# Gates, MoBA's queries and keys and cross attention's queries and keys as one 512-column matmul per weight tile

## What is computed

```
h = rmsnorm(x)
q_a,k_a,v_a, q_b,k_b,v_b, z, xbc, dt = split(h @ w_in)
y_a = sliding window attention(q_a,k_a,v_a)      # RoPE, sinks
y_b = MoBA attention(q_b,k_b,v_b)                # one block of 256: causal
y_c = SSD mixer(z, xbc, dt)                      # conv, scan, gated norm
g_a,g_b,g_c = split(sigmoid(h @ w_gate + b_gate))
x += (g_a*(y_a@w_br_a) + g_b*(y_b@w_br_b) + g_c*(y_c@w_br_c)) @ w_mix_out
q = rmsnorm(x) @ w_cq;  k,v = split(rmsnorm(mem) @ w_ckv)
x += softmax(q k^T) v @ w_co                     # 4 heads, 256 memory tokens
x += relu(rmsnorm(x) @ w_up)^2 @ w_down
```

## Time and profile before

| | us |
|---|---|
| median of 3 runs | 1207.43 (1206.92 to 1207.82) |
| the profiled execution, its time | 1205.99 |
| the same, span of the profile | 1204.2 |
| PE busy | 1168.9 (97%) |
| PE weight loads busy | 1047.6 (87%) |
| DVE busy | 774.5 (64%) |
| ACT busy | 573.3 (48%) |
| POOL busy | 66.1 (5%) |

### The profile page before, as it was taken

One profiled execution on the slowest core, in us unless ns is written; L12 is line 12 of the kernel. 1 busy time (PEld: TensorE's weight loads), 2 busy tenths in 40 slices (PEclk: granted clock), 3 DMA queues, 4 the chain that ended last, 5 costly groups with the idle time before them and its releaser, 6 DMA issues. The chain is left out here.

```text
span 1204.2 us, 18337 instructions
## 1 busy us (share of the span) xinstructions
PE 1168.9 (97%) x7503; PEld 1047.6 (87%) x7503; DVE 774.5 (64%) x1172; ACT 573.3 (48%) x808; POOL 66.1 (5%) x93
## 2 busy tenths in 40 slices
PE   4999999999999999999999999999999999999997
PEld 3998899999998887888889888999989988888886
DVE  5877765886654456656568677568685445655655
ACT  5545454534554355344355545544455444534443
POOL 2000001410000000000000000043000000000000
PEclk9999999999999999999999999999999999999999
DMA  5743525746643445655636533366655443575560
GB/s 183 229 156 110 171 71 179 232 137 218 199 165 133 154 148 188 210 175 176 209 109 209 175 126 120 112 186 193 204 182 190 152 148 105 175 243 168 190 220 36
DMA packets 156412, 201.31 MB, mean 167 GB/s; under 512 B 7152, under 2 KB 111912, under 8 KB 156328
## 3 DMA queue, kind: packets, MB, share of 16 engines
q1 hardware_dynamic: 155296, 199.46, 51.0%
q10 hardware_dynamic: 1032, 0.67, 0.2%
HBM read 199.04 MB, written 1.08 MB: 166 GB/s over the span
## 5 line engine op out<-in xcount | busy, mean ns | idle before, releaser
L1401 DVE TENSOR_TENSOR w_lo<-raw,w_hi 128x2048 fp32r<-128x2048 f32 (+1 forms) x184 | 412.5, 2245 | 249.6 <-ACT w_hi L742 249.5
L742 ACT ACTIVATE w_hi<-raw 128x2048 fp32r<-128x2048 f32 (+1 forms) x184 | 343.2, 1875 | 108.4 <-PE psum L1114 78.5
L1097 PE MATMUL psum<-act_both,w_hi 128*128 128x256 f32 x832 | 240.9, 290 | 0.0
L1099 PE MATMUL psum<-act_both,w_lo 128*128 128x256 f32 x832 | 235.2, 283 | 0.0
L1098 PE MATMUL psum<-act_both,w_hi 128*128 128x256 f32 x832 | 235.2, 283 | 0.0
L1085 PE MATMUL psum<-act_both,w_hi 128*128 128x512 f32 x512 | 181.8, 399 | 2.3 <-DVE w_lo L1401 2.3
L1097 PEld LDWEIGHTS psum<-act_both,w_hi 128*128 128x128 f32 x832 | 159.3, 191 | 1.1 <-issue 0.5
L1098 PEld LDWEIGHTS psum<-act_both,w_hi 128*128 128x128 f32 x832 | 159.4, 192 | 0.6 <-issue 0.5
L1099 PEld LDWEIGHTS psum<-act_both,w_lo 128*128 128x128 f32 x832 | 159.2, 191 | 0.0
L1086 PE MATMUL psum<-act_both,w_lo 128*128 128x256 f32 x512 | 143.5, 280 | 0.0
L1085 PEld LDWEIGHTS psum<-act_both,w_hi 128*128 128x128 f32 x512 | 96.1, 188 | 27.2 <-DVE w_lo L1401 3.1
(11 more groups left out here) (252 smaller groups left out, 1923.9 us busy)
## 6 DMA issues: line engine op xcount, KB each, us to landing
raw<-in_w_in_dram SPq DMA_DIRECT2D x35, 1024.0 KB, 5.0
raw<-in_w_up_dram SPq DMA_DIRECT2D x32, 1024.0 KB, 5.4
raw<-in_w_down_dram SPq DMA_DIRECT2D x32, 1024.0 KB, 4.9
raw<-in_w_gate_dram SPq DMA_DIRECT2D x24, 1024.0 KB, 7.1
raw<-in_w_ckv_dram SPq DMA_DIRECT2D x16, 1024.0 KB, 5.2
raw<-in_w_br_ssd_dram SPq DMA_DIRECT2D x8, 1024.0 KB, 10.0
raw<-in_w_mix_out_dram SPq DMA_DIRECT2D x8, 1024.0 KB, 5.0
raw<-in_w_cq_dram SPq DMA_DIRECT2D x8, 1024.0 KB, 5.3
```

The costliest lines, as they stand in the source:

```text
L742: act.activation(w_hi[:, slot, 0:n], raw[:, slot, 0:n], ACT.Copy).then_inc(hi_ready.sem, 1)
L1097: pe.matmul(dst, m_hi[:, k, cs], a_hi[:, k, :], start=k == 0, stop=False)
L1099: ins = pe.matmul(dst, m_lo[:, k, cs], a_hi[:, k, :], start=False, stop=k == kt - 1)
L1401: dve.tensor_tensor(w_lo[:, slot, 0:n], raw[:, slot, 0:n], w_hi[:, slot, 0:n].bitcast(F32), ALU.subtract).then_inc(lo_ready.sem, 1)
```

## The change

Four kinds of unit, 24 of them per layer (`qkb` 4, `gate` 12, `kx` 4, `qx` 4), take the form of the up-projection: 16 pairs of matmuls (512 columns and 256) in place of 48 matmuls of 256 columns, and two banks per unit in place of one. After such a unit ACT copies the second halves of both banks into the destination (for a gate it adds half the bias and multiplies by 0.5 on the way), DVE adds the first halves (two instructions of 256 columns) and frees both banks. A gate's tanh is a third instruction on ACT, of 512 columns in SBUF, and comes after `hi` of the unit three further on and before the exponentials of the slot. `xbc` and `branch_c` keep the old form. The two halves of the memory's activations become one tile at the same place.

```diff
+MERGED = ('qkb', 'gate', 'kx', 'qx')
 def unit_banks(u, w):
...
-    if w["kind"] == "up":
+    if w["kind"] == "up" or w["kind"] in MERGED:
         return [(u, m) for m in range(2)]
...
+        hm_both = at("hm_both", [P, 2, KT, SEQ], F32R, r_c)
+        hm_hi, hm_lo = hm_both[:, 0], hm_both[:, 1]
...
                 act.wait_ge(*unit_done.at(l, u + 1))
-                if kind == "qkb":
+                if kind in MERGED:
+                    if kind == "gate":
+                        branch, tile = w["col"] // D, (w["col"] % D) // P
+                        if branch == 1:
+                            act.wait_ge(*is_read(l, (U_BRA + 1, 1)))
+                        if branch == 2:
+                            act.wait_ge(*is_read(l, (U_BRB + 1, 1)))
+                    for m in range(2):
+                        src = bank((u, m))[:, SEQ:2 * SEQ]
+                        if kind == "gate":
+                            b0 = PC_BGATE + branch * KT + tile + m
+                            ins = act.activation(g_sb[:, tile + m, :], src, ACT.Identity, bias=half[:, l, b0:b0 + 1],
+                                                 scale=0.5)
+                        else:
+                            dst = {"qkb": qkT_b, "kx": k_xT, "qx": q_xT}[kind]
+                            ins = act.activation(dst[:, 2 * j + m, :], src, ACT.Copy)
+                    ins.then_inc(half_out.sem, 1)
+                elif kind == "qkb":
...
                     if u + RING < NU and w["kind"] != "xbc":
                         hi(l, u + RING)
+                    if w["kind"] == "gate" and "gate" in MERGED:
+                        c = (w["col"] % D) // P
+                        for m in range(2):
+                            act.wait_ge(*is_read(l, (u, m)))
+                        act.activation(g_sb[:, c:c + 2, :], g_sb[:, c:c + 2, :], ACT.Tanh).then_inc(gate_out.sem, 1)
...
+                elif w["kind"] in MERGED:
+                    both = hm_both if w["act"] == "mem" else act_both
+                    for m in range(2):
...
+                            pe.matmul(dst, m_hi[:, k, cs], both[:, :, k, :], start=k == 0, stop=False)
                             ins = pe.matmul(dst[:, 0:SEQ], m_lo[:, k, cs], a_hi[:, k, :], start=False,
                                             stop=k == kt - 1)
...
+                if kind in MERGED:
+                    n = merged_until(u)
+                    dve.wait_ge(*half_out.at(l, n))
+                    for m in range(2):
+                        src = bank((u, m))[:, 0:SEQ]
+                        if kind == "gate":
+                            dst = g_sb[:, (w["col"] % D) // P + m, :]
+                            ins = dve.scalar_tensor_tensor(dst, src, 0.5, dst, ALU.mult, ALU.add)
+                        else:
+                            dst = {"qkb": qkT_b, "kx": k_xT, "qx": q_xT}[kind][:, 2 * j + m, :]
+                            ins = dve.tensor_tensor(dst, dst, src, ALU.add)
+                        ins.then_inc(free((u, m)), 1)
+                    return
```

More of the change, by code:

```diff
@@ L360, in trunk @@
         yc_lo = at("yc_lo", [P, KT, SEQ], F32R, r_c + 8192)
-        hm_hi = at("hm_hi", [P, KT, SEQ], F32R, r_c)
-        hm_lo = at("hm_lo", [P, KT, SEQ], F32R, r_c + 8192)
+        hm_both = at("hm_both", [P, 2, KT, SEQ], F32R, r_c)
+        hm_hi, hm_lo = hm_both[:, 0], hm_both[:, 1]
         r_d = region(8192)
@@ L478, in trunk @@
         close_hi = Signal(sem("close_hi"), 8)
+        n_merged = sum(w["kind"] in MERGED for w in UNITS)
+        gate_out = Signal(sem("gate_out"), 12)
+        half_out = Signal(sem("half_out"), n_merged)
         mg_ready = Signal(sem("mg_ready"), 4)
@@ L571, in prev_user, with merged_until @@
             return u - RING
+        def merged_until(u):
+            return sum(w["kind"] in MERGED for w in UNITS[:u + 1])
         def unit_bank(u, i):
@@ L1027, in _ @@
             operands = {"h": (act_hi, act_lo), "merged": (act_hi, act_lo), "hq": (act_hi, act_lo),
-                        "hf": (act_hi, act_lo), "mem": (hm_hi[:], hm_lo[:]), "o": (o_hi[:], o_lo[:]),
+                        "hf": (act_hi, act_lo), "mem": (hm_hi, hm_lo), "o": (o_hi[:], o_lo[:]),
                         "y_swa": (ya_hi[:], ya_lo[:]), "y_moba": (yb_hi[:], yb_lo[:]),
@@ L1085, in unit @@
                             pe.matmul(dst, m_hi[:, k, cs], act_both[:, :, k, :], start=k == 0, stop=False)
+                            ins = pe.matmul(dst[:, 0:SEQ], m_lo[:, k, cs], a_hi[:, k, :], start=False,
+                                            stop=k == kt - 1)
+                elif w["kind"] in MERGED:
+                    both = hm_both if w["act"] == "mem" else act_both
+                    for m in range(2):
+                        if m == 1:
+                            inner(l, u)
+                        dst, cs = bank(unit_bank(u, m)), slice(m * P, (m + 1) * P)
+                        for k in range(kt):
+                            if turned and m == 0 and k % 2 == 0:
+                                pe.wait_ge(*is_read(l, ("norm", turned, k // 2)))
+                            pe.matmul(dst, m_hi[:, k, cs], both[:, :, k, :], start=k == 0, stop=False)
                             ins = pe.matmul(dst[:, 0:SEQ], m_lo[:, k, cs], a_hi[:, k, :], start=False,
@@ L1213, in job_scores @@
                 if n == 8:
-                    wait_read(pe, l, [(first_of("qkb", i), 0) for i in range(4)] + [unit_bank(U_VB, t) for t in range(TT)])
+                    wait_read(pe, l, [key for i in range(4) for key in unit_banks(first_of("qkb", i), UNITS[first_of("qkb", i)])] + [unit_bank(U_VB, t) for t in range(TT)])
                 for i in range(2):
@@ L1278, in cross_scores @@
                 key = ("xscore", h)
-                wait_read(pe, l, ([(U_KX + i, 0) for i in range(4)] if h == 0 else []) + [(U_QX + h, 0)])
+                wait_read(pe, l, [key for v in ([U_KX + i for i in range(4)] if h == 0 else []) + [U_QX + h]
+                                   for key in unit_banks(v, UNITS[v])])
                 pe.wait_ge(*is_free(l, key))
@@ L1628, in evacuate @@
                         if i == 0:
-                            wait_read(dve, l, [(v, 0) for v in range(u - 8, u) if UNITS[v]["kind"] == "gate"])
+                            if "gate" in MERGED:
+                                dve.wait_ge(*gate_out.at(l, 4 * (1 + ("branch_a", "branch_b", "branch_c").index(kind))))
+                            else:
+                                wait_read(dve, l, [(v, 0) for v in range(u - 8, u) if UNITS[v]["kind"] == "gate"])
                         if kind == "branch_a":
```

## The result

The changed kernel takes 1212.05 us (median of 6 executions) against 1207.09 for the kernel before beside it; the ratio is 1.0040, 95% interval 1.0026 to 1.0054. It is 0.4% slower. One of the six executions took 1641.11 us at a granted clock of 0.657 and is not in the ratio; the other five have a median of 1211.30 and a mean of 1211.84. The profiled execution took 1211.1 us with a span of 1209.3, where the one of before took 1205.99 with a span of 1204.2.

A forecast was written before the change was run, and what follows sets the result against it. The prediction took PE to bound the kernel. Per layer, waits of 0.85 + 2.6 us less 2.6 saved gave +0.85, so +1.7 for two layers on the 1207.43 us median: 1209.1 us, range 1204.6 to 1214.0.

The forecast's parts named there:

- The likeliest case: Both bank waits come and outweigh the savings: 1209.1 us, own range 1205.2 to 1211.5, chance 0.56.
- wait at `kva`: After unit 2, `kva` needs both `qa` banks and waits for the second token tile's RoPE copy: 0.85 us per layer.
- later start of unit 34, from unit 29 on: Bank wait for `branch_b1`, DVE's additions and a share for POOL meetings: 2.6 us per layer, between 2.27 and 3.6.
- savings of the other units: Twenty units per layer, all but 2, 29, 30 and 33, each save 0.13 us: 2.6 us.
- two paces: Up-projection units take 5.55 or 5.65 us; the saving per changed unit was put between 0.07 and 0.21 us.
- Unit 34's bank wait: Unit 34 needs banks 2 and 3 and waits for DVE's last read of `branch_b1`: 2.27 us computed per layer.
- the bank alone: At unit 34, the wait for bank 3 even with nothing later on DVE: 1.46 us.
- the late exponentials: In slots 28 and 29 tanh waits for DVE's additions, shifting exponentials and POOL's multiplication; a meeting costs about 1.30 us.
- SSD's chain becomes the bound: Exponentials wait behind tanh and POOL's multiplications fall on DVE's masks: 4.9 us slower, 1212.3 us, chance 0.30.
- one meeting before, at the scaling: In the kernel before, POOL's slot 28 multiplication overlapped DVE's `y_tok` scaling: 1.30 us beside 1.51.
- two rivals: Slower ones: SSD's chain as bound, 1212.3 us, chance 0.30; PE's time by columns alone, 1214.3 us, chance 0.05.
- the gap rule: On PE, N/2.4 ns plus 2.5 ns between successive matmuls; by it a merged unit would save 0.04 us.

The follow-up runs named there:

- e6: Changed kernel plus unread matmuls filling PE's pauses before unit 34, 18 before the turning of `y_tok` and 8 behind it; 1207.20 us, ratio 0.9994 to the kernel before.
- e10: Changed kernel with the gates of units 33 and 34 in old form and 18 unread matmuls before the turning of `y_tok`; 1204.55 us, ratio 0.9981.
- e7: e6 with ACT's tanh of a gate moved behind the exponentials of its slot; 1206.04 us, ratio 0.9993 to the kernel before.
- e12: Changed kernel run once more without any edit; 1212.14 us, ratio 1.0033 to the kernel before.
- e3: Changed kernel with the gates of units 33 and 34 in their old form; 1207.46 us, ratio 1.0001 to the kernel before.
- e1: Kernel before with only `kx` and `qx` in the new form, 8 units per layer; 1206.31 us, ratio 0.9982.
- e4: Changed kernel with the gates of units 28, 29 and 30 in their old form; 1209.94 us, ratio 1.0022 to the kernel before.
- e9: Kernel before plus 10 unread matmuls per layer before the turning of `y_tok`; 1205.83 us, ratio 0.9984 to the kernel before.

## Why the prediction was right or wrong

The range of 1204.6 to 1214.0 held the result. The likeliest case has its time at its very upper edge: its range ends at 1211.5, the median of all six is 1212.05, that of the five is 1211.30. By the prediction's own measure of 0.2% the kernel is slower, and that had 0.42 against 0.49 for the same. The time lies near that of a rival, 1212.3, mostly for a reason the rival does not have, so that the nearness is luck. By its steps:

| per layer, us | predicted | e6 (clock up) | changed, first run |
|---|---|---|---|
| wait at `kva` | 0.85 | 0.95 / 0.95 | 0.95 / 0.95 |
| later start of unit 34, from unit 29 on | 2.6 | 2.46 / 2.22 | 2.69 / 3.42 |
| unit 34 at the lower clock | none | 0 / 0 | 1.28 / 1.30 |
| savings of the other units | -2.6 | -2.24 / -2.48 | -2.13 / -2.50 |
| net, from unit 2 to the layer's end | 0.85 | 1.17 / 0.69 | 2.79 / 3.17 |

Each entry is read from the starts of units in the traces, in which unit 34 of the first run is 1.17 and 1.19 us longer and lacks the 0.11 it should have saved; the savings are what is left of the net.

*The saving*, 0.13 us per unit, was right in kind: 0.11 to 0.13 over the 20 units. The two paces seen in `up` exist in the changed units too, and which one a unit gets is still open.

*The wait at `kva`* was right to 0.1 us; the difference is the handshake, 0.14 us where 0.05 was taken. The first matmul behind the wait takes 0.36 us where it took 0.29.

*Unit 34's bank wait* was right in mechanism and, with the clock up, in size: computed 2.27, taken 2.6, measured 2.34 on average. Within it the prediction's 1.46 for the bank alone stands against 1.63 (e10 against e6). DVE's read of bank 3 ended at 252.43 + 0.68 = 253.11, which is 0.87 us later than before if both are counted from unit 28; 0.81 was predicted. But e7 shows that this delay is not DVE's additions alone; through POOL's meetings with the masks the late exponentials have a share, which the sum had as 0.3 us.

*The rival "SSD's chain becomes the bound"* is true in part. POOL's multiplications meet masks more often, as it said. (The prediction counted one meeting before, at the scaling; the mask of slot 31 had one too, with 2.17 us in both layers.) In the second layer the masks of slots 28 to 31 (L1748) took 2.17, 2.17, 2.16 and 2.17 us where they took 1.14, 2.16, 1.41 and 2.17 before. The meeting of slot 30, and the turning that follows it:

```profile
820.43 2.02 POOL L698 TENSOR_TENSOR s_sb<-s_sb,cbT 128x512 f32<-128x512 f32 x1 [3.96 <-ACT s_sb L882]
821.23 2.16 DVE L1748 SCALAR_TENSOR_TENSOR s_sb<-pT_sb,acs,mask_ssd 128x128 f32<-128x128 f32 x4
826.94 0.66 PE L1317 MATMUL psum<-ident,y_tok 128*128 128x128 f32 x4 [0.30 <-DVE y_tok L1812]
```

That layer then lost 0.85 us at the start of unit 32, which is the third wait for `y_tok`. e12 shows it in the second layer and e3 in the first, e6 in neither. It goes with the mask of slot 28, which takes 2.17, 2.03 and 2.18 us in the three layers with the loss and 1.14 to 1.38 in the other layers of these four traces. In the three POOL begins its multiplication of slot 27 5.5 to 6.2 us after the start of unit 28 and is still at it when that mask begins, in the others after 4.2 to 4.9 us. What makes POOL late in some executions is open.

*What failed* is what the sum left out. It priced every wait at its length. The prediction itself had PE idle "some 4 us together" at unit 34, and did not ask what the granted clock does then; it asked nothing of the 1.44 us between the profiled execution and the median either. Both have one answer. The profiled execution of before was one of those that kept their clock (0.999), most do not, and the changed kernel never keeps it. With the clock held up the net is 1.86 us by the trace of e6 and 1.6 by its executions at 0.999, against the 1.7 of the prediction. By the ratio e6 is even 0.7 us under the kernel before, since that reference has the low clock in it too: its 87 executions lie on average 1.4 us above those at 0.999. The changed kernel lies 4.7 to 5.6 us above e6 (e12 and the first run, by the ratios). Not all of the 4.7 to 5.6 is the clock. The first trace's net is 4.1 us above that of e6, of which 2.6 lie inside unit 34 and 1.4 in its later start; for e12 it is 5.5, with 5.0 and 0.8, and the rest is in the savings. The later start is for the most part the loss at unit 32, which comes ahead of the fall of the clock. So the term that was missing is the low clock behind the pauses, 2.6 to 5.0 us in the two layers by the traces.

That the range held without this term is owed to its upper part, which was there for two rivals. The prediction's use of the gap rule needs a correction too: the Trainium skill (TensorE: Matmul & The Clock Gate, Back-to-back issue gap) gives that formula for a single matmul by itself and not for a stream with a weight load for each. So the 120 ns of the earlier trace rows do not speak against it; the sum does not use it.

*Costed at nothing*: ACT's first copy of a gate took 0.47 us with its bias where 0.38 was assumed, and hid as expected: no wait of PE is put down to it. DVE's additions took 0.416 us, as in the up-projection.

```profile
L1637 DVE SCALAR_TENSOR_TENSOR g_sb<-psum,g_sb 128x256 f32<-128x256 f32 x48 | 18.0, 416 | 4.0 <-ACT g_sb L825 4.0
L825 ACT ACTIVATE g_sb<-psum,half 128x256 f32<-128x256 f32 x48 | 20.1, 474 | 15.2 <-PE psum L1129 14.9
```

## What to carry to other kernels

A wait on TensorE can have two prices: its length, and the lower clock of the work behind it, 0.9 to 2.6 us for one unit of 1 MB here. Price both, and look at the mean clock of every execution before taking a profiled one as the reference. A form that saves 0.12 us per unit is worth taking only for the units where a bank is free and DVE has time; here 18 of 24 made the kernel 0.42% faster and all 24 made it 0.4% slower.

## What the hardware showed that I had not expected

- The granted clock fell to 0.50 after PE had idled 2.7 us in one piece (e1 and e3) as well as after 2.72 + 1.35 us, with the four small matmuls of a turning between them, and after 2.13 + 1.35 us (e4). In the profile of before, pauses of 1.74 and 2.02 us in the same place did not bring it down, though other executions of that kernel lost it.
- Work that computes nothing made a kernel faster: ten matmuls in a pause of each layer, 0.16% on the kernel before (e9), and 26 per layer about 0.4% on the changed one (e6).
- At half clock a pair of matmuls started every 0.64 us, against 0.35 us at full clock, so 1.8 times, not twice.
